# Residual stages of a two-block model: the first step's weights split in two pieces, the source split moved

## The chip, the cores and the metric

The kernel runs on one core of one Trainium2 chip. The metric is the device time in microseconds. TensorE does the matmuls, VectorE, ScalarE and GpSimd the elementwise work, and SyncE issues the loads.

## The reference

The reference is one forward pass over 512 tokens of width 1024, in float32, through two blocks in a row. The first has two layers: a mixer (attention with forgetting and differential heads in layer 0, an mLSTM in layer 1), a cross attention over 256 memory rows and a convolutional feed-forward network of width 2816. The second is a modulated block with a recurrent mixer (rwkv7 and RG-LRU) and a mixture of 32 experts. What matters here is the form in which each of these parts comes back into the residual stream:

```python
x = x + mixed @ w_out                                    # mixers of layers 0 and 1
x = x + cross @ wo[layer]                                # cross attentions
x = x + hidden @ w_down[layer]                           # feed-forward networks, 2816 rows
x = x + gt1[:, None, :] * (merged @ w_out[l])            # second block, gated
mod = c_act @ w_ada[l] + b_ada[l]                        # modulation: 64 columns of 128 values, from one row c
```

## The kernel before, in words

All activations are kept feature-major: 128 partitions, 8 tiles of 512 tokens. The program is a sequence of stages, each a block in which every engine has its own instruction stream; a stage begins for all engines when the one ahead has ended. `stage_dense_residual` (line 449) runs seven times: behind the attention, the mLSTM and the two cross attentions (`src` is `mix`, 8 steps), behind the two feed-forward networks (`src` is `hidden`, 22 steps, `columns` given), and behind the merge of the second block (`src` is `merged`, 8 steps, `gate` given).

A step is one tile of 128 source rows. Its weights are 128x1024 and its source 128x512. TensorE multiplies in a rounded type (float32r), so each operand is split in a rounded half (`hi`) and the rest (`lo`), and each product is three matmuls: hi by hi, hi by lo, lo by hi (`split_products`, lines 220 to 222). A step has 8 output banks and so 24 matmuls of 128x512.

Per step k, on buffer k % 2: ScalarE waits until TensorE has finished step k-2 (`used`) and until the weights have landed, then rounds the weights (line 508) and the source (line 509). GpSimd waits for the rounded weights and makes their rest (line 517). The source's rest (line 478) is VectorE's in the stages without modulation, and GpSimd's, behind the weights' rest, in the two with it. TensorE waits for both rests. SyncE loads the weights of step k once the weights' rest of step k-2 is made (`w_split`). The first and the last round of two steps are written out, the others are in a loop.

Beside the two feed-forward stages runs the `Modulation` (line 1579): 33 and 31 rows of 128x1024 are loaded into three places, and VectorE multiplies each by the row c and sums (line 1619). SyncE's queue issues them in a fixed order: weights of the even step, two rows, weights of the odd step, one row. Before, ScalarE applies Silu to c, behind its work for the first two steps. When all is done, VectorE adds each bank to x (line 553, gated 555).

Of the kernel before, what the change touches and what calls it, by code (L numbers as in the profile page):

```python
# [19 lines left out]
ACT = mybir.ActivationFunctionType  # L20
ALU = mybir.AluOpType
# [5 lines left out]
P = 128  # L27
T = 512
D = 1024
# [81 lines left out]
def first_loads(sp, units):  # L111

    if units is not None:
        for s in range(units.per):
            units.load(sp, 0, s)
# [102 lines left out]
def split_products(nc, out, left, right, first, last):  # L218

    nc.tensor.matmul(out, left.hi, right.hi, start=first, stop=False)  # L220
    nc.tensor.matmul(out, left.hi, right.lo, start=False, stop=False)  # L221
    return nc.tensor.matmul(out, left.lo, right.hi, start=False, stop=last)  # L222
# [226 lines left out]
def stage_dense_residual(g, units, coming, src, gate=None, columns=None):  # L449


    nc = g.nc
    units.begin()
    rounds = units.n
    with ExitStack() as ctx:
        sem, sb = g.stage(ctx, f"dense{units.base[0]}")
        w_rounded, s_rounded, w_split, s_split, used, done, read, passed = (
            sem(n) for n in ("w_rounded", "s_rounded", "w_split", "s_split", "used", "product_done", "bank_read", "passed"))
        w = [Split(sb(f"w_hi{b}", [P, D], F32R), sb(f"w_lo{b}", [P, D], F32R)) for b in range(2)]
        s = [Split(sb(f"s_hi{b}", [P, T], F32R), sb(f"s_lo{b}", [P, T], F32R)) for b in range(2)]  # L460
        beside = Modulation(g, ctx, *columns) if columns else None
        block = ctx.enter_context(nc.Block())

        def steps(eng, step, between=None):

            def both(i):
                for b in range(2):
                    k = 2 * i + b
                    step(i, b, k, slice(k, k + 1) if isinstance(i, int) else bass.ds(k, 1))
            both(0)  # L470
            if between:
                between(eng)
            with eng.Fori(1, rounds - 1) as i:
                both(i)
            both(rounds - 1)

        def rest_of_source(eng, b, tile):
            eng.tensor_tensor(s[b].lo[:, :], src[:, tile, :].rearrange("p a n -> p (a n)"), s[b].hi[:, :],  # L478
                              ALU.subtract).then_inc(s_split, 1)

        @block.sync
        def _(sp):
            def both(i, more=()):
                for b in range(2):
                    sp.wait_ge(w_split, 2 * i + b - 1)
                    units.load(sp, i, b)
                    for s in more[2 * b:2 * b + 2]:
                        beside.load(sp, i, s)
            if beside:
                places = range(beside.PLACES)  # L490
                beside.first_loads(sp)
                with sp.Fori(1, beside.rounds) as i:
                    both(i, places)
                for i in range(beside.rounds, rounds):
                    both(i, places[0:beside.n - beside.PLACES * i])
            else:
                with sp.Fori(1, rounds) as i:
                    both(i)
            sp.wait_ge(w_split, 2 * rounds)
            first_loads(sp, coming)  # L500

        @block.scalar
        def _(act):
            def step(i, b, k, tile):
                if not isinstance(i, int) or i > 0:
                    act.wait_ge(used, k - 1)
                units.wait(act, i, b)
                nc.scalar.activation(w[b].hi[:, :], units.rows(b, 0, D, 0, D), ACT.Copy).then_inc(w_rounded, 1)  # L508
                nc.scalar.activation(s[b].hi[:, :], src[:, tile, :].rearrange("p a n -> p (a n)"), ACT.Copy).then_inc(s_rounded, 1)  # L509
            steps(act, step, beside.scalar if beside else None)  # L510

        @block.gpsimd
        def _(pool):
            def step(i, b, k, tile):
                pool.wait_ge(w_rounded, k + 1)
                pool.sem_inc(passed, 1)
                nc.gpsimd.tensor_tensor(w[b].lo[:, :], units.rows(b, 0, D, 0, D), w[b].hi[:, :], ALU.subtract).then_inc(w_split, 1)  # L517
                if beside:
                    pool.wait_ge(s_rounded, k + 1)
                    pool.sem_inc(passed, 1)  # L520
                    rest_of_source(nc.gpsimd, b, tile)
            steps(pool, step)

        @block.tensor
        def _(pe):
            def step(i, b, k, tile):
                first = isinstance(i, int) and k == 0
                last = isinstance(i, int) and k == 2 * rounds - 1
                pe.wait_ge(w_split, k + 1)
                pe.wait_ge(s_split, k + 1)  # L530
                for m in range(KT):
                    mm = split_products(nc, g.bank[m][:, :], w[b].cut(m * P, (m + 1) * P), Split(s[b].hi[:, :], s[b].lo[:, :]), first, last)
                    if last:
                        mm.then_inc(done, 1)
                if not last:
                    mm.then_inc(used, 1)
            steps(pe, step)

        @block.vector
        def _(dve):  # L540
            def step(i, b, k, tile):
                dve.wait_ge(s_rounded, k + 1)
                dve.sem_inc(passed, 1)
                rest_of_source(nc.vector, b, tile)
            if beside:
                beside.vector(dve)
            else:
                steps(dve, step)
            for m in range(KT):
                dve.wait_ge(done, m + 1)  # L550
                here = g.x[:, m, :]
                if gate is None:
                    nc.vector.tensor_tensor(here, g.bank[m][:, :], here, ALU.add).then_inc(read, 1)
                else:
                    nc.vector.scalar_tensor_tensor(here, g.bank[m][:, :], gate[:, m:m + 1], here, ALU.mult, ALU.add).then_inc(read, 1)
            if beside:
                beside.end(dve)
# [2534 lines left out]
def build(nc, A, where, out):  # L3092

    with ExitStack() as ctx:
        g = Core(nc, ctx, A, where)
        U = {name: Units(g.ring, A[name]) for name in A if name.startswith("w_")}
        stage_setup(g, U["w_attn"])
        stage_attention(g, U["w_attn"], U["w_attn_out"])
        stage_dense_residual(g, U["w_attn_out"], U["w_xattn0"], g.mix)
        for layer in range(2):  # L3100
            if layer == 1:
                stage_mlstm(g, U["w_mlstm"], U["w_mlstm_out"])
                stage_dense_residual(g, U["w_mlstm_out"], U["w_xattn1"], g.mix)
            stage_cross_attention(g, U[f"w_xattn{layer}"], U[f"w_xattn_out{layer}"], layer)
            stage_dense_residual(g, U[f"w_xattn_out{layer}"], U[f"w_up{layer}"], g.mix)
            with nc.sbuf_tensor(f"hidden{layer}", [P, FT, T], F32) as hidden:
                stage_ffn_up(g, U[f"w_up{layer}"], U[f"w_down{layer}"], layer, hidden)
                stage_dense_residual(g, U[f"w_down{layer}"], U[("w_mlstm", "w_rec_in")[layer]], hidden,
                                     columns=((0, 33), (33, 31))[layer])
# [34 lines left out]
```

## Time and profile before

| | |
|---|---|
| median of 3 runs | 2915.34 us (2911.96 to 2918.43) |
| profiled execution, its own time | 2913.45 us |
| its span | 2911.6 us, 38111 instructions |
| TensorE matmuls | 2553.2 us busy (88%) |
| VectorE | 1212.1 us (42%) |
| ScalarE | 957.0 us (33%) |
| GpSimd | 981.3 us (34%) |
| lines 220 to 222 of the residual stages | 672 matmuls each, 270.5 + 266.8 + 266.5 us |

The span is the time from the first to the last instruction of one profiled execution, and its own time is that of the same run measured outside. Busy time of TensorE counts overlapping matmuls, whose ends are modelled, so 88% is not a share of its peak.

### The profile page before, as it was taken

The numbers are of one execution on the slowest core, as the hardware profiler recorded it, in microseconds if no ns is written. First come the engines' busy times: TensorE is split into PE (matmuls) and PEld (weight loads), VectorE is DVE, ScalarE is ACT, GpSimd is POOL, SyncE is SP. The second block draws the span as 40 slices with busy tenths as digits, with TensorE's granted clock in tenths as the row PEclk, the third lists the DMA queues.
The fourth block names the chain that finished last, engine by engine and source line by source line (L and its number), as shares of the span: only waits on it lengthen the run. The fifth ranks groups of instructions, "written<-read, shape, count | busy, mean of one in ns | idle before, by whom it ended". The sixth has DMA issues, their size and how long they took to land. (4 is left out here: it accounts for less than half of the span.)

```text
span 2911.6 us, 38111 instructions
## 1 busy us (share of the span) xinstructions
PE 2553.2 (88%) x14762; PEld 1857.3 (64%) x14762; DVE 1212.1 (42%) x1578; ACT 957.0 (33%) x1362; POOL 981.3 (34%) x469
## 2 busy tenths in 40 slices
PE   8998898899898899789889989889887798579996
PEld 5776786688775666568668877667576586223334
DVE  5443523566554433352256655432644414311112
ACT  4443422444423333243244442243422322201113
POOL 5221422343375311142234337532121342223321
PEclk9999899899998888899989999989999899689998
DMA  3111221222264111122122326422001122598992
GB/s 122 66 44 51 94 87 58 96 91 101 97 227 152 44 43 43 36 105 90 54 91 86 101 80 233 149 72 79 2 4 46 54 77 80 214 370 330 370 349 97
DMA packets 76277, 333.84 MB, mean 115 GB/s; under 512 B 17113, under 2 KB 21209, under 8 KB 51801
## 3 DMA queue, kind: packets, MB, share of 16 engines
q1 hardware_dynamic: 62336, 313.98, 29.7%
q0 software_dynamic: 13824, 18.19, 1.8%
q8 instruction: 87, 1.43, 0.2%
q14 instruction: 30, 0.25, 0.0%
HBM read 372.67 MB, written 16.78 MB: 134 GB/s over the span
## 5 line engine op out<-in xcount | busy, mean ns | idle before, releaser
L517 POOL TENSOR_TENSOR dense_w_lo<-weights,dense_w_hi 128x1024 fp32r<-128x1024 f32 x84 | 203.1, 2420 | 468.4 <-ACT dense_w_hi L508 468.4
L220 PE MATMUL bank<-dense_s_hi,dense_w_hi 128*128 128x512 f32 x672 | 270.5, 402 | 63.5 <-DVE dense_s_lo L478 35.5
L221 PE MATMUL bank<-dense_s_lo,dense_w_hi 128*128 128x512 f32 x672 | 266.8, 397 | 0.0
L222 PE MATMUL bank<-dense_s_hi,dense_w_lo 128*128 128x512 f32 x672 | 266.5, 397 | 0.0
L508 ACT ACTIVATE dense_w_hi<-weights 128x1024 fp32r<-128x1024 f32 x84 | 88.9, 1058 | 345.4 <-PE bank L222 318.7
L220 PEld LDWEIGHTS bank<-dense_s_hi,dense_w_hi 128*128 128x128 f32 x672 | 129.6, 193 | 104.6 <-POOL dense_w_lo L517 39.3
L1276 DVE TENSOR_TENSOR hidden<-up_y 128x512 f32 x44 | 158.2, 3594 | 64.6 <-ACT up_y L1238 64.0
L222 PE MATMUL bank<-xn_r,weights_r 128*128 128x512 f32 x448 | 177.0, 395 | 0.0
L1619 DVE SCALAR_TENSOR_TENSOR xn<-mix,xn 128x1024 f32<-128x1024 f32 x64 | 123.1, 1923 | 118.0 <-DMA mix<-in_modulation 104.6
L2777 PE MATMUL bank<-moe_weights,mix 128*64 128x512 f32 x320 | 151.9, 628 | 17.5 <-DMA experts_more_up<-in_experts_up,moe_more_up 17.3
L1253 POOL TENSOR_TENSOR mix_r<-weights,mix_r 128x2048 fp32r<-128x2048 f32 x22 | 101.3, 4605 | 162.3 <-ACT mix_r L1226 162.3
L220 PE MATMUL bank<-xn_r,mix_r 128*128 128x512 f32 x352 | 141.8, 403 | 8.3 <-DVE up_xn_lo_r L317 8.1
L1253 POOL TENSOR_TENSOR up_w_lo<-weights,up_w_hi 128x2048 fp32r<-128x2048 f32 x22 | 101.3, 4605 | 136.0 <-ACT up_w_hi L1226 136.0
L222 PEld LDWEIGHTS bank<-dense_s_hi,dense_w_lo 128*128 128x128 f32 x672 | 129.2, 192 | 27.9
L221 PEld LDWEIGHTS bank<-dense_s_lo,dense_w_hi 128*128 128x128 f32 x672 | 129.8, 193 | 26.2
L222 PE MATMUL bank<-xn_r,mix_r 128*128 128x512 f32 x352 | 140.2, 398 | 0.0
L221 PE MATMUL bank<-up_xn_lo_r,mix_r 128*128 128x512 f32 x352 | 139.8, 397 | 0.0
L222 PE MATMUL bank<-xn_r,up_w_lo 128*128 128x512 f32 x352 | 139.6, 396 | 0.0
L220 PE MATMUL bank<-xn_r,up_w_hi 128*128 128x512 f32 x352 | 139.0, 395 | 0.0
L221 PE MATMUL bank<-up_xn_lo_r,up_w_hi 128*128 128x512 f32 x352 | 137.4, 390 | 0.0
L2777 PE MATMUL bank<-experts_more_up,mix 128*64 128x512 f32 x256 | 123.3, 638 | 5.1 <-DMA experts_more_up<-in_experts_up,moe_more_up 5.1
L478 DVE TENSOR_TENSOR dense_s_lo<-mix,dense_s_hi 128x512 fp32r<-128x512 f32 x32 | 78.2, 2452 | 112.1 <-ACT dense_s_hi L509 112.1
(637 smaller groups left out, 6082.3 us busy)
## 6 DMA issues: line engine op xcount, KB each, us to landing
weights<-in_w_up SPq DMA_DIRECT2D x44, 1024.0 KB, 4.8
moe_weights<-in_experts_up SPq DMA_DIRECT2D x40, 1024.0 KB, 14.5
mix<-in_modulation SPq DMA_DIRECT2D x64, 512.0 KB, 4.6
weights<-in_w_xattn SPq DMA_DIRECT2D x24, 1024.0 KB, 4.9
weights<-in_experts_up SPq DMA_DIRECT2D x24, 1024.0 KB, 9.4
weights<-in_w_down SPq DMA_DIRECT2D x44, 512.0 KB, 3.7
moe_weights<-in_experts_down SPq DMA_DIRECT2D x40, 512.0 KB, 9.2
weights<-in_w_attn SPq DMA_DIRECT2D x8, 1536.0 KB, 6.6
```

The lines of the kernel that those rows point to most:

```text
L220: nc.tensor.matmul(out, left.hi, right.hi, start=first, stop=False)
L221: nc.tensor.matmul(out, left.hi, right.lo, start=False, stop=False)
L222: return nc.tensor.matmul(out, left.lo, right.hi, start=False, stop=last)
L478: eng.tensor_tensor(s[b].lo[:, :], src[:, tile, :].rearrange("p a n -> p (a n)"), s[b].hi[:, :], ALU.subtract).then_inc(s_split, 1)
L508: nc.scalar.activation(w[b].hi[:, :], units.rows(b, 0, D, 0, D), ACT.Copy).then_inc(w_rounded, 1)
L517: nc.gpsimd.tensor_tensor(w[b].lo[:, :], units.rows(b, 0, D, 0, D), w[b].hi[:, :], ALU.subtract).then_inc(w_split, 1)
L1253: nc.gpsimd.tensor_tensor(w[s].lo, units.rows(s, 0, KT * W, 0, KT * W), w[s].hi, ALU.subtract).then_inc(w_split, 1)
L1276: nc.vector.tensor_tensor(h[:, bass.ds(2 * i + b // 2, 1), :], y[:, b - 1, :], y[:, b, :], ALU.mult).then_inc(h_done, 1)
L1619: g.nc.vector.scalar_tensor_tensor(self.product, self.rows[j % self.PLACES], 1.0, self.c, ALU.mult, ALU.mult, accum_out=g.mod[:, self.firs ...
L2777: mm = nc.tensor.matmul(g.bank[2 + n % 2][half, :], xt[n % 2][:, k, half], w[k // 4][:, k % 4 * 2 * FE:(k % 4 + 1) * 2 * FE], start=(k == ...
```

## The change

In every residual stage the first step is prepared in another order. ScalarE rounds the source first, and then the weights in two pieces, columns 0 to 255 and 256 to 1023 (`PIECES`). GpSimd makes the weights' rest piece by piece, each behind its own count (`w_first_rounded`, `w_first`), and then raises `w_split`. VectorE makes the source's rest, also in the two stages beside the modulation, where GpSimd did it before. TensorE waits for the source's rest (`s_first`) and for the first piece, and for the second piece at output bank 2.

In the later steps of the two stages beside the modulation, ScalarE rounds the source ahead of the weights, and GpSimd makes the source's rest ahead of the weights' rest. In the later steps of the other stages only the counts differ (`s_split` reaches one less, since the first step has its own).

```diff
--- before.py
+++ after.py
@@ -459,7 +459,12 @@
         w = [Split(sb(f"w_hi{b}", [P, D], F32R), sb(f"w_lo{b}", [P, D], F32R)) for b in range(2)]
         s = [Split(sb(f"s_hi{b}", [P, T], F32R), sb(f"s_lo{b}", [P, T], F32R)) for b in range(2)]
         beside = Modulation(g, ctx, *columns) if columns else None
+        w_first, w_first_rounded, s_first = sem("w_first"), sem("w_first_rounded"), sem("s_first")
+        PIECES = ((0, 2 * P), (2 * P, D))
         block = ctx.enter_context(nc.Block())
+
+        def source(tile):
+            return src[:, tile, :].rearrange("p a n -> p (a n)")
 
         def steps(eng, step, between=None):
 
@@ -474,9 +479,8 @@
                 both(i)
             both(rounds - 1)
 
-        def rest_of_source(eng, b, tile):
-            eng.tensor_tensor(s[b].lo[:, :], src[:, tile, :].rearrange("p a n -> p (a n)"), s[b].hi[:, :],
-                              ALU.subtract).then_inc(s_split, 1)
+        def rest_of_source(eng, b, tile, ready):
+            eng.tensor_tensor(s[b].lo[:, :], source(tile), s[b].hi[:, :], ALU.subtract).then_inc(ready, 1)
 
         @block.sync
         def _(sp):
@@ -501,24 +505,47 @@
 
         @block.scalar
         def _(act):
+            def round_source(b, tile):
+                nc.scalar.activation(s[b].hi[:, :], source(tile), ACT.Copy).then_inc(s_rounded, 1)
+
             def step(i, b, k, tile):
                 if not isinstance(i, int) or i > 0:
                     act.wait_ge(used, k - 1)
-                units.wait(act, i, b)
-                nc.scalar.activation(w[b].hi[:, :], units.rows(b, 0, D, 0, D), ACT.Copy).then_inc(w_rounded, 1)
-                nc.scalar.activation(s[b].hi[:, :], src[:, tile, :].rearrange("p a n -> p (a n)"), ACT.Copy).then_inc(s_rounded, 1)
+                if isinstance(i, int) and k == 0:
+                    round_source(b, tile)
+                    units.wait(act, i, b)
+                    for c0, c1 in PIECES:
+                        nc.scalar.activation(w[b].hi[:, c0:c1], units.rows(b, 0, D, c0, c1), ACT.Copy).then_inc(w_first_rounded, 1)
+                    act.sem_inc(w_rounded, 1)
+                elif beside:
+                    round_source(b, tile)
+                    units.wait(act, i, b)
+                    nc.scalar.activation(w[b].hi[:, :], units.rows(b, 0, D, 0, D), ACT.Copy).then_inc(w_rounded, 1)
+                else:
+                    units.wait(act, i, b)
+                    nc.scalar.activation(w[b].hi[:, :], units.rows(b, 0, D, 0, D), ACT.Copy).then_inc(w_rounded, 1)
+                    round_source(b, tile)
             steps(act, step, beside.scalar if beside else None)
 
         @block.gpsimd
         def _(pool):
             def step(i, b, k, tile):
-                pool.wait_ge(w_rounded, k + 1)
-                pool.sem_inc(passed, 1)
-                nc.gpsimd.tensor_tensor(w[b].lo[:, :], units.rows(b, 0, D, 0, D), w[b].hi[:, :], ALU.subtract).then_inc(w_split, 1)
-                if beside:
+                first = isinstance(i, int) and k == 0
+                if beside and not first:
                     pool.wait_ge(s_rounded, k + 1)
                     pool.sem_inc(passed, 1)
-                    rest_of_source(nc.gpsimd, b, tile)
+                    rest_of_source(nc.gpsimd, b, tile, s_split)
+                if first:
+                    for n, (c0, c1) in enumerate(PIECES):
+                        pool.wait_ge(w_first_rounded, n + 1)
+                        nc.gpsimd.tensor_tensor(w[b].lo[:, c0:c1], units.rows(b, 0, D, c0, c1), w[b].hi[:, c0:c1],
+                                                ALU.subtract).then_inc(w_first, 1)
+                    pool.wait_ge(w_first, len(PIECES))
+                    pool.sem_inc(w_split, 1)
+                else:
+                    pool.wait_ge(w_rounded, k + 1)
+                    pool.sem_inc(passed, 1)
+                    nc.gpsimd.tensor_tensor(w[b].lo[:, :], units.rows(b, 0, D, 0, D), w[b].hi[:, :], ALU.subtract).then_inc(w_split, 1)
             steps(pool, step)
 
         @block.tensor
@@ -526,9 +553,14 @@
             def step(i, b, k, tile):
                 first = isinstance(i, int) and k == 0
                 last = isinstance(i, int) and k == 2 * rounds - 1
-                pe.wait_ge(w_split, k + 1)
-                pe.wait_ge(s_split, k + 1)
+                if first:
+                    pe.wait_ge(s_first, 1)
+                else:
+                    pe.wait_ge(s_split, k)
+                    pe.wait_ge(w_split, k + 1)
                 for m in range(KT):
+                    if first and m * P in (c0 for c0, _ in PIECES):
+                        pe.wait_ge(w_first, [c0 for c0, _ in PIECES].index(m * P) + 1)
                     mm = split_products(nc, g.bank[m][:, :], w[b].cut(m * P, (m + 1) * P), Split(s[b].hi[:, :], s[b].lo[:, :]), first, last)
                     if last:
                         mm.then_inc(done, 1)
@@ -541,8 +573,9 @@
             def step(i, b, k, tile):
                 dve.wait_ge(s_rounded, k + 1)
                 dve.sem_inc(passed, 1)
-                rest_of_source(nc.vector, b, tile)
+                rest_of_source(nc.vector, b, tile, s_first if isinstance(i, int) and k == 0 else s_split)
             if beside:
+                step(0, 0, 0, slice(0, 1))
                 beside.vector(dve)
             else:
                 steps(dve, step)
```

## Rows read from the trace of the kernel before

**Rows 1.** The page's costliest groups, busy, mean ns, idle before and releaser:
```profile
L220 PE MATMUL bank<-dense_s_hi,dense_w_hi 128*128 128x512 f32 x672 | 270.5, 402 | 63.5 <-DVE dense_s_lo L478 35.5
```

**Rows 2.** Tile dense_s_hi, idle until: us, times.
```profile
  POOL dense_s_lo L478: 27.8, 22
```

**Rows 3.** Timeline behind the attention: start us, us, engine, line, idle before.
```profile
260.67 1.06 ACT L508 ACTIVATE dense_w_hi<-weights 128x1024 fp32r<-128x1024 f32 x1 [0.29 <-PEq L587]
261.63 0.61 ACT L509 ACTIVATE dense_s_hi<-mix 128x512 fp32r<-128x512 f32 x1
261.91 5.12 POOL L517 TENSOR_TENSOR dense_w_lo<-weights,dense_w_hi 128x1024 fp32r<-128x1024 f32 x2 [51.86 <-ACT dense_w_hi L508]
...
262.40 5.17 DVE L478 TENSOR_TENSOR dense_s_lo<-mix,dense_s_hi 128x512 fp32r<-128x512 f32 x2 [5.17 <-ACT dense_s_hi L509]
...
264.95 0.77 PE L220 MATMUL bank<-dense_s_hi,dense_w_hi 128*128 128x512 f32 x1 [5.20 <-DVE dense_s_lo L478]
```

**Rows 4.** Timeline, start of the gated stage.
```profile
2418.31 1.06 ACT L508 ACTIVATE dense_w_hi<-weights 128x1024 fp32r<-128x1024 f32 x1 [14.18 <-DMA weights<-in_w_mix_out]
...
2422.58 0.77 PE L220 MATMUL bank<-dense_s_hi,dense_w_hi 128*128 128x512 f32 x1 [7.99 <-DVE dense_s_lo L478]
```

**Rows 5.** Timeline, start of the first stage beside the modulation.
```profile
786.43 1.06 ACT L508 ACTIVATE dense_w_hi<-weights 128x1024 fp32r<-128x1024 f32 x1 [2.40 <-PEq L1179]
...
789.96 1.27 POOL L478 TENSOR_TENSOR dense_s_lo<-hidden,dense_s_hi 128x512 fp32r<-128x512 f32 x1
...
791.37 0.77 PE L220 MATMUL bank<-dense_s_hi,dense_w_hi 128*128 128x512 f32 x1 [8.68 <-POOL dense_s_lo L478]
791.87 2.77 DVE L1619 SCALAR_TENSOR_TENSOR xn<-mix,xn 128x1024 f32<-128x1024 f32 x1 [5.74 <-ACT xn L1610]
...
797.57 0.33 SPq L93 DMA_DIRECT2D weights<-in_w_down  x1
```

**Rows 6.** Timeline of ScalarE, two steps apart, behind the first cross attention.
```profile
478.75 1.06 ACT L508 ACTIVATE dense_w_hi<-weights 128x1024 fp32r<-128x1024 f32 x1 [8.41 <-PE bank L222]
...
489.63 1.06 ACT L508 ACTIVATE dense_w_hi<-weights 128x1024 fp32r<-128x1024 f32 x1 [3.95 <-PE bank L222]
```

**Rows 7.** Timeline of a later step beside the modulation.
```profile
834.56 1.06 ACT L508 ACTIVATE dense_w_hi<-weights 128x1024 fp32r<-128x1024 f32 x1 [4.90 <-PE bank L222]
...
835.80 2.39 POOL L517 TENSOR_TENSOR dense_w_lo<-weights,dense_w_hi 128x1024 fp32r<-128x1024 f32 x1 [1.78 <-ACT dense_w_hi L508]
...
837.24 2.03 DVE L1619 SCALAR_TENSOR_TENSOR xn<-mix,xn 128x1024 f32<-128x1024 f32 x1 [2.12 <-DMA mix<-in_modulation]
...
838.14 2.27 POOL L478 TENSOR_TENSOR dense_s_lo<-hidden,dense_s_hi 128x512 fp32r<-128x512 f32 x1
...
838.96 0.93 SPq L1606 DMA_DIRECT2D mix<-in_modulation  x2
...
840.55 0.47 PE L220 MATMUL bank<-dense_s_hi,dense_w_hi 128*128 128x512 f32 x1 [0.66 <-POOL dense_s_lo L478]
...
846.38 1.06 ACT L508 ACTIVATE dense_w_hi<-weights 128x1024 fp32r<-128x1024 f32 x1 [4.88 <-PE bank L222]
```

**Rows 8.** A 128x256 ScalarE activation (timeline); subtractions of line 317, ns min/median/max.
```profile
242.61 0.38 ACT L779 ACTIVATE attention_probs_T<-bank 128x256 f32<-128x256 f32 x1 [0.59 <-PE bank L698]
...
L317 DVE TENSOR_TENSOR xattn_xn_lo_r<-xattn_xn_lo,xn_r x8: 691/693/694, 336.9 to 1297.2; 128x512 fp32r<-128x512 f32 x8
```

**Rows 9.** Stretches: us, TensorE busy (x), granted clock, DMA share, GB/s.
```profile
260.00:264.92 4.92, 0.00 (x0) 0.78 0.00 0
264.92:269.70 4.78, 4.75 (x11) 0.51 0.66 201
...
466.40:471.58 5.18, 0.00 (x1) 0.94 0.00 0
```

**Rows 10.** Loads beside the modulation, KB each, median us to landing.
```profile
mix<-in_modulation SPq DMA_DIRECT2D x33, 512.0 KB, 4.7
weights<-in_w_down SPq DMA_DIRECT2D x20, 512.0 KB, 3.7
```

## The prediction

> **What bounds the kernel now.** I read the page's costliest groups first, then who waited for the source's rounded half, then the timeline at the start of each residual stage, then the clock by stretch, and last the timeline of two steps beside the modulation. The core works through stages one after another; a residual stage ends with its last matmul and the eight adds behind it, so a microsecond gained by TensorE in a stage is a microsecond of the span. TensorE stands at 88% of the span. The first of the three products of a residual stage (line 220) has 63.5 us of idle time ahead of it, 35.5 of them until VectorE's source rest is there [rows 1] and 27.8, in 22 times, until GpSimd's is there [rows 2]. These two are the waits on which the edit works.
>
> The 35.5 us are the starts of the five stages without modulation. Part of each idle time is the end of the stage ahead; what the stage itself costs is counted from ScalarE's first instruction. Behind the attention that is 260.67, and the first matmul is at 264.95: 4.28 us, in which ScalarE rounds 1024 columns of weights, then the source, GpSimd makes the weights' rest and VectorE the source's [rows 3]. In the gated stage the start is the arrival of the weights at 2418.31, and the matmul comes 4.27 us later [rows 4]. The 27.8 us are, in each of the two stages beside the modulation, one start of 8.68 us (4.94 of it behind ScalarE's first instruction, 786.43 to 791.37 [rows 5]) and ten later waits, 20 in both, of (27.8 - 17.4) / 20 = 0.52 us on average.
>
> These later waits come every second step. Without modulation two steps take 489.63 - 478.75 = 10.88 us, so 48 matmuls at 0.227 us [rows 6]. Beside it they take 846.38 - 834.56 = 11.82 us [rows 7]. The 0.94 us between them is the wait and a few slower matmuls behind it. The chain is short and visible: ScalarE starts at 834.56, GpSimd's weights at 835.80, its source rest at 838.14 lasting 2.27 us, the matmul at 840.55, so 5.99 us from ScalarE to TensorE, of which 1.0 us is not work: the same instruction took 1.27 us at 789.96, when VectorE was idle [rows 5], and here VectorE's modulation row stands from 837.24 to 839.27 across its start [rows 7]. GpSimd and VectorE take turns.
>
> **The change at the start of a stage without modulation.** Let ScalarE's first instruction stand at 0. Now the source is rounded first: 0.61 us. VectorE starts 0.16 us behind it (262.40 against 261.63 + 0.61 [rows 3]), at 0.77, and needs 0.69 us when GpSimd is idle, as the same subtraction of 128x512 does elsewhere [rows 8], so it is done at 1.46. In rows 3 two of them needed 5.17 us, since GpSimd was already at work when they began; here VectorE is there first. ScalarE starts the next instruction 0.10 us before the one ahead of it ends (261.63 against 260.67 + 1.06), so the piece of 256 columns stands at 0.51 and ends at 0.89, with the 0.38 us of another 128x256 activation [rows 8]. GpSimd could start 0.18 us later (261.91 against 261.73) at 1.07. I take it that it waits for VectorE until 1.46. Its price for 256 columns: 512 took 1.27 us [rows 5], 1024 took 2.39 [rows 7], so 2.1 to 2.2 ns a column and 0.2 fixed: 0.73 us for 256 and 1.8 for 768. The piece is there at 2.19, and TensorE starts 0.14 later, as at 791.23 to 791.37 [rows 5]: **2.33 instead of 4.28, 1.95 us less.** Four stages (behind the attention, the mLSTM and both cross attentions): 7.8 us. The bounds: GpSimd isn't held, 1.96 instead of 2.33 (2.3 less); or the small instruction has as much fixed time as the whole 128x512 one, 1.27 us, and is held as well (1.4 less).
>
> The row at 838.14 shows the turn-taking, and it bears on the order of the first two. The Trainium skill (page "SBUF — State Buffer", section "SBUF: two separate sides") calls the pair of ports that the two engines share an exclusive lock: whoever starts first keeps it for the whole instruction. By that rule GpSimd's first piece waits for 1.46; if the two merely shared it would not, and the sum for six starts would be 6 x 0.37 = 2.2 us larger.
>
> Does the second piece hold TensorE? It runs 2.2 to 4.05. The first six matmuls need only the first piece. The clock was at its lower level (1.2 GHz) in all of the first 4.78 us of this stage, 11 matmuls at 0.43 us [rows 9], so six last 2.6 us, to 4.9: no wait. At 2.4 GHz they last 1.4, to 3.7, and TensorE waits 0.4. Step two: its source rest and then its weights' rest follow on GpSimd until some 7.1, and TensorE needs them at 2.33 + 7.4 or, with the upper clock, at 8.2: hidden. The weights of step three are asked for when the first rest is whole, at 4.2 (before at 3.8), land 3.7 us later [rows 10] at 7.9 and are needed behind step one, at 8.0 at the earliest (2.33 + 5.45 and ScalarE's start): hidden, at the upper clock barely.
>
> **In the gated stage** the source is rounded and its rest made before the weights land; nothing holds GpSimd. From the landing: 0.38 + 0.18 + 0.73 + 0.14 = 1.43 instead of 4.27, **2.8 us less**.
>
> **The starts beside the modulation.** GpSimd had weights' rest and source rest of step one in a row. The source rest goes to VectorE, idle until 791.87 [rows 5]: 2.33 instead of 4.94, **2.6 us less, twice 5.2**. What is moved: VectorE's first row, behind ScalarE's Silu at 5.4, now meets GpSimd's weights' rest of step two (5.4 to 7.8) instead of its source rest, and is perhaps 0.8 us later; the next load of weights on SyncE's queue stands behind that row's reload, at 797.57 [rows 5], and lands near 801.3, while step four's ScalarE work would be due at about 801.9 with TensorE 2.6 us earlier. Hidden, by little; if not, up to 1 us a stage.
>
> **The later steps beside the modulation.** From ScalarE's start, without a row of VectorE in between: 0.61 + 0.18 + 1.27 + 2.40 + 0.14 = 4.6 us. Before, the same sum was 1.06 + 0.18 + 2.40 + 1.27 + 0.14 = 5.05. The matmul at 840.55 started 0.66 + 0.39 = 1.05 us behind the one ahead of it instead of 0.23, so it lost 0.82, and without a wait it would stand 5.99 - 0.82 = 5.17 us behind ScalarE's start; the other 0.12 of the 0.94 us are the slower matmuls behind the wait. With one modulation row in the way (1.0 us) the new chain is 5.6: a wait of 0.43 instead of 0.82. With none, no wait. With a row ahead of each of GpSimd's two instructions, 6.6: worse than now. So it hangs on when rows land. A row's reload is issued some 0.75 us behind the end of the weights' rest, the weights' own load between them (838.96 against 835.80 + 2.39 [rows 7]), and lands 4.7 us after issue [rows 10]. The weights' rest is now the last link, so everything shifts. Counting from a step's ScalarE start (period 5.45): rest whole at 4.5, first row issued at 5.2, landed at 9.9, which is 4.45 in the next step, under the last of GpSimd's weights' rest; it then runs 1.23 us up to 0.25 in the step behind, before GpSimd's source rest at 0.79. The second of the pair lands some 1.4 us later and runs into that source rest, holding it by about 0.8: chain 5.4, a wait of 0.25 and the slower matmuls' 0.12 once in two steps. The third row finds room. So 0.57 of the 0.94 us goes, ten times in each of two stages: **11.4 us**. Bounds: 0 (a row ahead of the weights' rest each time, late by 0.4 more than I count) to 0.94 (no row in the way), 0 to 19 us. The weights' load comes 0.9 us later in the step and has over 2 us of slack before ScalarE needs it.
>
> **The clock.** Idle time ahead of the stage behind the first cross attention was 5.2 us, with the granted clock at 0.94 on average, so the lower level came only in its last 0.6 us; behind the attention it was 0.78, the last 2.2 us [rows 9]. With 1.95 us less of idleness the first could keep 2.4 GHz: ten matmuls 0.2 us faster, less the 0.4 us wait for piece two, 1.6. Three of the seven stages have so short an idle time, so 0 to 5 us; I take 1. The Trainium skill ("TensorE: Matmul & The Clock Gate", Part 1) says that the monitor runs free of the program, so where the level changes varies from run to run; by it this term is luck in every stage. The 0.6 and 2.2 us of two like stages agree.
>
> **The sum.** 7.8 + 2.8 + 5.2 + 11.4 + 1.0 = 28.2 us. The profiled execution took 2913.45 us around a span of 2911.6, 1.9 under the median of 2915.34; it would come to 2885.3, and the median to **2887**. No other stage is touched, and each starts as before, only earlier. What a measurement of this kernel can tell from no change is about 0.2%, 5.8 us.
>
> **Rivals.**
> 1. The starts gain, the later steps don't: rows land ahead of GpSimd's second instruction, chain 6.0 as before. Gain 10 to 19, about 2900. For it: my count of landings is good to perhaps 0.5 us, and 0.4 decides. Chance 0.20.
> 2. All later waits go and the clock stays up: 7.8 + 2.8 + 5.2 + 18.8 + 4 = 38.6, about 2877. For it: the uncontended chain has half a microsecond to spare. Against it: VectorE holds 3 x 1.23 of each 10.9 us. Chance 0.15.
> 3. Slower: GpSimd now has two places per step where VectorE can slip in ahead of something that TensorE waits for. Where all three rows of two steps hit, one step waits 6.6 - 5.17 = 1.4, the other 0.4, and 0.12 for each: 2.0 instead of 0.94, times 20 = 21 us lost against 16 gained at the starts: 2920. It decides from 0.94 + 15.8 / 20 = 1.7 us of waiting in two steps. Against it: in the row at 837.24 one landing hits one instruction, and three rows that land 1.4 to 5 us apart seldom all do. Chance 0.05.
> 4. It doesn't do what it says: GpSimd keeps the pair when its piece is ready, or small instructions are dear, so that the starts give under 1 us and the steps nothing: within 0.2%. Chance 0.05.
>
> The forecast itself, a gain of 19 to 36, has 0.55. Range: 2868 to 2904, which leaves out rivals 3 and 4 and the far ends of 1 and 2. Faster by over 0.2%: 0.89 (forecast, rivals 1 and 2, less 0.01 for the low end); same 0.06; slower 0.05.
>
> **What would show it.** In the starts: the first matmul 2.3 us after ScalarE's first instruction, 1.4 behind the landing in the gated stage; VectorE's rest of 0.69 us ahead of GpSimd's first piece. In the steps: two steps in 11.2 to 11.3 us instead of 11.82, and the wait now put down to the weights' rest. If two steps take 11.8 or more, the landings are what failed; if the starts show over 3 us, the prices of the pieces or the turn-taking are.

## The result, and the profile after

The changed kernel took 2892.58 us (median of 5 runs, 2887.71 to 2897.01) against 2915.34 (5 runs): a ratio of 0.992, 95% interval 0.9908 to 0.9931, so 22.8 us less. The profiled execution has a span of 2890.4 us against 2911.6. The direction and the starts of the stages came as forecast; the later steps beside the modulation gave a third of what was forecast.

The time of each residual stage, from ScalarE's first instruction (in the gated stage from the landing of its weights) to the end of the last add, read from the two timelines in us ("less" is what the stage became shorter by):

| stage behind | first matmul, before | after | stage, before | after | less |
|---|---|---|---|---|---|
| attention | 4.28 | 2.20 | 50.98 | 48.13 | 2.85 |
| cross attention 0 | 4.28 | 2.20 | 50.13 | 48.02 | 2.11 |
| feed-forward 0 (modulation) | 4.94 | 2.19 | 136.94 | 132.36 | 4.58 |
| mLSTM | 4.28 | 2.20 | 50.72 | 48.02 | 2.70 |
| cross attention 1 | 4.27 | 2.19 | 50.76 | 47.11 | 3.65 |
| feed-forward 1 (modulation) | 4.95 | 2.19 | 135.80 | 131.04 | 4.76 |
| merge (gated) | 4.27 | 1.36 | 50.86 | 48.46 | 2.40 |

That is 23.0 us; the span fell by 21.2, so the stages that the change doesn't touch took 1.8 longer in this execution.

In the page's costliest groups, the first product now waits for GpSimd's first pieces (line 541) where it waited for VectorE [rows 1]; 63.5 us of idle time became 43.6:

```profile
L220 PE MATMUL bank<-dense_s_hi,dense_w_hi 128*128 128x512 f32 x672 | 269.7, 401 | 43.6 <-POOL dense_w_lo L541 36.2
```

The timeline behind the attention answers to rows 3. VectorE's rest takes 0.69 us, since it is ahead of GpSimd; the two pieces (one row, x2) start at 261.55, and TensorE 1.19 us behind that. The two rows at the end are the first piece by itself, here and in the gated stage:

```profile
260.54 0.63 ACT L509 ACTIVATE dense_s_hi<-mix 128x512 fp32r<-128x512 f32 x1 [0.29 <-PEq L620]
261.07 1.13 ACT L518 ACTIVATE dense_w_hi<-weights 128x256 fp32r<-128x256 f32 x2
...
261.32 0.69 DVE L483 TENSOR_TENSOR dense_s_lo<-mix,dense_s_hi 128x512 fp32r<-128x512 f32 x1 [4.22 <-ACT dense_s_hi L509]
261.55 2.82 POOL L541 TENSOR_TENSOR dense_w_lo<-weights,dense_w_hi 128x256 fp32r<-128x256 f32 x2 [51.65 <-ACT dense_w_hi L518]
...
262.74 0.77 PE L220 MATMUL bank<-dense_s_hi,dense_w_hi 128*128 128x512 f32 x1 [3.12 <-POOL dense_w_lo L541]
...
261.55 1.04 POOL L541 TENSOR_TENSOR dense_w_lo<-weights,dense_w_hi 128x256 fp32r<-128x256 f32 x1 [51.65 <-ACT dense_w_hi L518]
2399.70 0.73 POOL L541 TENSOR_TENSOR dense_w_lo<-weights,dense_w_hi 128x256 fp32r<-128x256 f32 x1 [19.24 <-ACT dense_w_hi L518]
```

Behind the second cross attention the clock stayed up, and the second piece was late there: the weight load (PEld) of the third bank waited for it for 0.53 us, and the matmul started 0.49 us behind the one ahead of it (1412.16) instead of 0.23:

```profile
1410.94 0.47 PE L220 MATMUL bank<-dense_s_hi,dense_w_hi 128*128 128x512 f32 x1 [3.11 <-POOL dense_w_lo L541]
...
1412.65 0.19 PEld L220 LDWEIGHTS bank<-dense_s_hi,dense_w_hi 128*128 128x128 f32 x1 [0.53 <-POOL dense_w_lo L541]
```

A usual pair of later steps beside the modulation answers to rows 7. VectorE's row at 829.04 stands ahead of GpSimd's source rest at 829.17, which takes 2.24 us instead of 1.29; the chain from 828.28 to 833.80 is 5.52 us. Two steps take 839.68 - 828.28 = 11.40 us, where they took 11.82:

```profile
828.28 0.63 ACT L509 ACTIVATE dense_s_hi<-hidden 128x512 fp32r x1 [4.34 <-PE bank L222]
...
829.04 1.23 DVE L1652 SCALAR_TENSOR_TENSOR xn<-mix,xn 128x1024 f32<-128x1024 f32 x1 [0.51 <-DMA mix<-in_modulation]
829.17 2.24 POOL L483 TENSOR_TENSOR dense_s_lo<-hidden,dense_s_hi 128x512 fp32r<-128x512 f32 x1 [2.23 <-ACT dense_s_hi L509]
...
831.37 2.38 POOL L548 TENSOR_TENSOR dense_w_lo<-weights,dense_w_hi 128x1024 fp32r<-128x1024 f32 x1
...
833.80 0.50 PE L220 MATMUL bank<-dense_s_hi,dense_w_hi 128*128 128x512 f32 x1 [0.22 <-POOL dense_w_lo L548]
...
839.68 0.63 ACT L509 ACTIVATE dense_s_hi<-hidden 128x512 fp32r x1 [4.38 <-PE bank L222]
```

But three of the nine pairs of feed-forward 0 took 12.3 or 12.4 us (none of feed-forward 1 took over 11.7). In the first of them a row of VectorE is ahead of both of GpSimd's instructions (2.21 us for the source's rest, 3.35 for the weights'), and TensorE waits 1.17 us:

```profile
792.88 1.23 DVE L1652 SCALAR_TENSOR_TENSOR xn<-mix,xn 128x1024 f32<-128x1024 f32 x1
793.05 2.21 POOL L483 TENSOR_TENSOR dense_s_lo<-hidden,dense_s_hi 128x512 fp32r<-128x512 f32 x1 [2.70 <-ACT dense_s_hi L509]
...
795.11 1.23 DVE L1652 SCALAR_TENSOR_TENSOR xn<-mix,xn 128x1024 f32<-128x1024 f32 x1 [0.99 <-DMA mix<-in_modulation]
795.22 3.35 POOL L548 TENSOR_TENSOR dense_w_lo<-weights,dense_w_hi 128x1024 fp32r<-128x1024 f32 x1
...
798.62 0.50 PE L220 MATMUL bank<-dense_s_hi,dense_w_hi 128*128 128x512 f32 x1 [1.17 <-POOL dense_w_lo L548]
```

The groups of GpSimd in feed-forward 0 give the sum of the holds, that is, of the time by which VectorE made its instructions longer (busy us, mean ns). Before, the held instruction was the source's rest alone:

```profile
L517 POOL TENSOR_TENSOR dense_w_lo<-weights,dense_w_hi 128x1024 fp32r<-128x1024 f32 x22 | 52.8, 2399 | 50.0 <-ACT dense_w_hi L508 50.0
L478 POOL TENSOR_TENSOR dense_s_lo<-hidden,dense_s_hi 128x512 fp32r<-128x512 f32 x22 | 46.0, 2092 | 0.0
```

After, both are:

```profile
L548 POOL TENSOR_TENSOR dense_w_lo<-weights,dense_w_hi 128x1024 fp32r<-128x1024 f32 x21 | 57.0, 2716 | 0.0
L483 POOL TENSOR_TENSOR dense_s_lo<-hidden,dense_s_hi 128x512 fp32r<-128x512 f32 x21 | 38.7, 1842 | 27.1 <-ACT dense_s_hi L509 26.9 <-POOL dense_w_lo L541 0.3
```

Against what the two cost when VectorE leaves them alone (2401 and 1293 ns, e3 below), GpSimd was held 22 x 0.80 = 17.6 us before and 21 x (0.32 + 0.55) = 18.1 after. There the change moved the holds and took none away. In feed-forward 1 the same sum went from 15.6 us (22 of 2403 and 2001 ns) to 12.7 (21 of 2623 and 1674).

### The profile page after: what moved, and what is told of

It reads as the page before. It is cut to its first block and busy times, and to the rows that moved or that the text cites. A ratio compares the mean times of both kernels' runs of the same rounds, so it can differ in the third digit from the quotient of the medians.

```text
span 2890.4 us, 38084 instructions
## 1 busy us (share of the span) xinstructions
PE 2551.0 (88%) x14762; PEld 1857.5 (64%) x14762; DVE 1172.4 (41%) x1580; ACT 958.5 (33%) x1369; POOL 978.5 (34%) x474
## 5 line engine op out<-in xcount | busy, mean ns | idle before, releaser
L220 PE MATMUL bank<-dense_s_hi,dense_w_hi 128*128 128x512 f32 x672 | 269.7, 401 | 43.6 <-POOL dense_w_lo L541 36.2
L548 POOL TENSOR_TENSOR dense_w_lo<-weights,dense_w_hi 128x1024 fp32r<-128x1024 f32 x77 | 196.6, 2554 | 97.1 <-ACT dense_w_hi L526 95.7
L1652 DVE SCALAR_TENSOR_TENSOR xn<-mix,xn 128x1024 f32<-128x1024 f32 x64 | 100.2, 1566 | 134.1 <-DMA mix<-in_modulation 124.2
L1265 ACT ACTIVATE up_y<-bank,vecs 128x512 f32<-128x512 f32 x88 | 68.5, 779 | 169.3 <-PE bank L222 159.2
L541 POOL TENSOR_TENSOR dense_w_lo<-weights,dense_w_hi 128x256 fp32r<-128x256 f32 (+1 forms) x14 | 19.5, 1411 | 293.8 <-ACT dense_w_hi L518 293.8
```

The costliest lines, as they stand in the source:

```text
L541: nc.gpsimd.tensor_tensor(w[b].lo[:, c0:c1], units.rows(b, 0, D, c0, c1), w[b].hi[:, c0:c1], ALU.subtract).then_inc(w_first, 1)
L1265: nc.scalar.activation(y[:, b, :], g.bank[b][:, :], ACT.Identity, scale=tap(2, i, b), bias=tap(3, i, b)).then_inc(now_done, 1)
L1652: g.nc.vector.scalar_tensor_tensor(self.product, self.rows[j % self.PLACES], 1.0, self.c, ALU.mult, ALU.mult, accum_out=g.mod[:, self.firs ...
```

## The experiments

Theory A says that the starts made nearly all of the gain, and that VectorE's rows, in GpSimd's way, kept the later steps from giving more. Theory B says that the two parts gave shares as forecast. Rivals C and D are stated where they are tested. e1 to e4 ran beside one set of runs of the kernel before (2914.80 us), e5 to e7 beside another (2917.29).

What was expected of each run stands in front of its result, as it was written before the run.

**e1, the starts alone**, and **e2, the order alone**, each one part of the change (excerpts, with notes behind #; the expectation of e1 comes first):

```diff
 e1, from the kernel after:                       # ScalarE and GpSimd, steps k > 0
-                elif beside:
-                    round_source(b, tile)        # source ahead of weights
...
 e2, from the kernel before:
+                source_ahead = beside and not (isinstance(i, int) and k == 0)
+                if source_ahead:                 # ScalarE: source, weights; GpSimd likewise
```

> Only the first steps are changed; the later steps beside the modulation keep the order of before (weights, then source, on ScalarE and GpSimd). Theory A (the starts made nearly all of the 22.8 us, the later steps some 4): 2915.3 - 19 = 2896 us, and two later steps beside the modulation take 11.8 us as before. Theory B (the two parts gave about equal shares, as 16.8 to 11.4 in the forecast): 2915.3 - 13 = 2902. Both: first matmul 2.2 us behind ScalarE's first instruction in six stages.

> The kernel before, with only the order of source and weights turned in the later steps beside the modulation; all first steps as before. Theory A: a gain of 2 to 5 us (about 2911), two steps mostly in 11.4 us, with single pairs of 12 and more where VectorE's rows stand ahead of both of GpSimd's instructions. Theory B: a gain of 10 us, 2905.

e1: 2897.75 us, ratio 0.9938 (0.9921 to 0.9955), 18 us less by the ratio (13 to 23). e2: 2908.47 us, ratio 0.9982 (0.9971 to 0.9992), 5 us less (2 to 8). The parts add up to the whole (18 + 5 = 23), as far as intervals of 5 and 3 us to each side can tell, and in the shares of theory A. Theory B's 13 us for e1 stand at the edge of its interval; it is e2 that leaves out theory B's 10 us, and the 11.4 of the forecast.

The expectation for e1's pairs held only in part. Most took 11.7 to 11.9 us, three 12.1 to 12.3, and one of feed-forward 0 15.3. Two things met in it. With the rows nearly back to back, GpSimd's instructions were held one after the other (weights' rest 3.35 us, source rest 2.26), and TensorE waited 2.45 us at 807.22. And from 808.54 to 811.95 TensorE was at 1.2 GHz (granted clock 0.50, last row), ten matmuls that cost about 1.6 us more than at 2.4. ScalarE then waited 8.15 us:

```profile
807.06 3.35 POOL L540 TENSOR_TENSOR dense_w_lo<-weights,dense_w_hi 128x1024 fp32r<-128x1024 f32 x1
...
810.05 1.43 DVE L1648 SCALAR_TENSOR_TENSOR xn<-mix,xn 128x1024 f32<-128x1024 f32 x1 [1.87 <-DMA mix<-in_modulation]
810.37 2.26 POOL L483 TENSOR_TENSOR dense_s_lo<-hidden,dense_s_hi 128x512 fp32r<-128x512 f32 x1
...
814.63 1.06 ACT L522 ACTIVATE dense_w_hi<-weights 128x1024 fp32r<-128x1024 f32 x1 [8.15 <-PE bank L222]
...
807.22 0.49 PE L220 MATMUL bank<-dense_s_hi,dense_w_hi 128*128 128x512 f32 x1 [2.45 <-POOL dense_s_lo L483]
...
808.54:811.95 3.41, 3.41 (x10) 0.50 0.29 95
```

In that execution feed-forward 0 was 2.0 us longer than before (138.94 against 136.94) although its first matmul was 2.75 us earlier. In e2, where TensorE starts as late as before, all eighteen pairs of the two stages took 11.3 to 11.6 us. The 19 later steps, from ScalarE's start in the third to that in the last, took in the two stages:

| kernel | start | order | feed-forward 0 | feed-forward 1 |
|---|---|---|---|---|
| before | late | old | 111.87 | 111.26 |
| e1 | early | old | 116.15 | 112.40 |
| e2 | late | new | 108.04 | 108.47 |
| after | early | new | 110.79 | 108.55 |

So in feed-forward 0 the earlier start made the later steps longer, by 4.3 us with the old order (about 1.6 of it by the clock, as above) and by 2.8 with the new. The single pairs of 12 us that I expected in e2 are not there; in feed-forward 0 they are where the start was moved forward. Each of these figures is from one profiled execution. GpSimd was held less in e2, too: 12.0 us in feed-forward 0 (22 of 2564 and 1675 ns) and 13.2 in feed-forward 1 (2699 and 1597).

**e3, short rows**: VectorE's rows keep their loads and waits, but compute 64 of 1024 columns.

```diff
-            g.nc.vector.scalar_tensor_tensor(self.product, self.rows[j % self.PLACES], 1.0, self.c, ...
+            g.nc.vector.scalar_tensor_tensor(self.product[:, 0:64], self.rows[j % self.PLACES][:, 0:64], 1.0, self.c[:, 0:64], ...
```

> The kernel after, with VectorE's modulation instructions cut to the first 64 of their 1024 columns (this leaves out most of the modulation sums); all loads, waits and counts stay. Theory A (VectorE's rows hold the SBUF access from GpSimd, and that is the rest of the loss in the later steps): two steps beside the modulation in 10.9 us, 19 steps some 7 us shorter in each of the two stages, so 2892.6 - 14 = 2879. Rival C (what holds the later steps is the landing of the loads, which keep their size): two steps stay at 11.4 us, 2890 to 2893.

The 19 later steps took 103.26 us in both stages, pairs of 10.9 throughout, and GpSimd's two instructions their bare time:

```profile
L548 POOL TENSOR_TENSOR dense_w_lo<-weights,dense_w_hi 128x1024 fp32r<-128x1024 f32 x21 | 50.4, 2401 | 0.0
L483 POOL TENSOR_TENSOR dense_s_lo<-hidden,dense_s_hi 128x512 fp32r<-128x512 f32 x21 | 27.2, 1293 | 36.8 <-ACT dense_s_hi L509 36.5 <-POOL dense_w_lo L541 0.3
```

The two stages are 7.9 and 5.3 us shorter than in the kernel after, 13.2 for the 14 expected, with the loads the same in number and size, if not in time: rival C (the loads) falls. The time as a whole, 2859.65 us, fell by 33, more than the stages explain: what follows the gated stage took 426.2 us of the span instead of 442.7. The incomplete modulation sums go into the router, and the work of the experts depends on values; that this is the cause of the 16.5 us is inferred, not shown, so e3 is read by its two stages alone.

**e4, the source's rest on VectorE in every step**, between its rows, with ScalarE's weights first again (VectorE's part of the edit):

```diff
-                step(0, 0, 0, slice(0, 1))
-                beside.vector(dve)
+                for k in range(2 * rounds):
+                    step(k // 2, k % 2, k, slice(k, k + 1))
+                    if k == 1:
+                        dve.wait_ge(beside.silu_ready, 1)
+                        beside.multiply(dve, range(0, 3))
+                    elif k > 1:
+                        j = 3 * (k // 2) + 2 * (k % 2)
+                        beside.multiply(dve, range(j, min(j + 2 - k % 2, beside.n)))
```

> The kernel after, but in the two stages beside the modulation VectorE makes the source's rest in every step, between its rows (two rows behind the rest of an even step, one behind that of an odd step), and ScalarE rounds the weights first again. GpSimd has only the weights' rest. Chain of GpSimd from ScalarE's start 1.06 + 0.18 + 2.39 + 0.14 = 3.8 us, 4.9 with one row ahead of it, under the 5.2 us that it has. Theory A: two steps in 10.9 us, 2892.6 - 13 = 2880. Rival C (loads): no gain. Rival D (VectorE comes late to the source's rest, because it stands behind a row that has not landed): two steps over 11.4 us, 2893 or more.

2880.29 us (2877.82 to 2883.79), ratio 0.9881 (0.9867 to 0.9896). The forecast of 2880 held. In the pair shown, GpSimd is ahead and takes 2.40 us, as in nearly every step; VectorE's rest waits for it (2.46 us) and is done at 830.56, before TensorE wants it. Pairs are 837.26 - 826.38 = 10.88 us:

```profile
826.38 1.06 ACT L522 ACTIVATE dense_w_hi<-weights 128x1024 fp32r<-128x1024 f32 x1 [3.95 <-PE bank L222]
...
827.61 2.40 POOL L540 TENSOR_TENSOR dense_w_lo<-weights,dense_w_hi 128x1024 fp32r<-128x1024 f32 x1 [3.13 <-ACT dense_w_hi L522]
828.10 2.46 DVE L483 TENSOR_TENSOR dense_s_lo<-hidden,dense_s_hi 128x512 fp32r<-128x512 f32 x1 [1.92 <-ACT dense_s_hi L509]
...
837.26 1.06 ACT L522 ACTIVATE dense_w_hi<-weights 128x1024 fp32r<-128x1024 f32 x1 [3.94 <-PE bank L222]
```

The stages are 124.60 and 124.44 us, as short as with short rows (124.43, 125.77), with all the work done, and TensorE waits ahead of none of their later steps. So the holds fell on the path only because GpSimd had two instructions in the chain. Rival D falls too.

**e5, one piece**: source first, VectorE ahead, but the weights whole.

```diff
-        PIECES = ((0, 2 * P), (2 * P, D))
+        PIECES = ((0, D),)
```

> The kernel after with the first step's weights in one piece of 1024 columns; the source still goes first and its rest to VectorE. Theory A (the piece is what brings the start forward, since GpSimd's 1024 columns of 2.4 us stand last in the chain): first matmul 0.51 + 1.06 + 0.18 + 2.39 + 0.14 = 4.3 us behind ScalarE's first instruction in six stages, as much as before; 2892.6 + 6 x 2.1 + 2.4 = 2907 us. Rival B (the order, source first and VectorE ahead of GpSimd, brings it): first matmul 2.2 to 2.8 us, 2893 to 2897.

2903.75 us, ratio 0.9953 (0.9939 to 0.9966). The first matmul is 4.14 us behind ScalarE's first instruction in six stages, so without the piece the start is not brought forward to 2.20:

```profile
260.81 0.63 ACT L509 ACTIVATE dense_s_hi<-mix 128x512 fp32r<-128x512 f32 x1 [0.28 <-PEq L620]
...
262.46 2.34 POOL L541 TENSOR_TENSOR dense_w_lo<-weights,dense_w_hi 128x1024 fp32r<-128x1024 f32 x1 [52.19 <-ACT dense_w_hi L518]
...
264.95 0.77 PE L220 MATMUL bank<-dense_s_hi,dense_w_hi 128*128 128x512 f32 x1 [5.06 <-POOL dense_w_lo L541]
```

The order alone gives 0.14 us in four stages, 0.8 in the two beside the modulation (4.95 before) and 0.65 in the gated one (3.62 behind the landing). Pieces in the old order were not run, so what they give without the source going first is not shown.

The time is 3 us under the expected 2907. With the later start nearly every pair beside the modulation was regular again (19 steps in 108.23 and 107.86 us), as in e2, while I had counted on those of the kernel after.

**e6, three pieces on top of e4**:

```diff
-        PIECES = ((0, 2 * P), (2 * P, D))
+        PIECES = ((0, P), (P, 3 * P), (3 * P, D))
```

> The kernel of e4 (VectorE makes the source's rest in every step) with the first step's weights in three pieces: 128, 256 and 640 columns. Theory A: a piece of 128 columns costs GpSimd 0.46 us, is ready at 0.28 + 0.51 + 0.18 = 0.97 and held by VectorE until 1.46: first matmul at 1.46 + 0.46 + 0.14 = 2.06 or a little less, instead of 2.20, and 1.1 instead of 1.36 in the gated stage; 7 x 0.2 = 1.4 us less, which the trace shows and the times hardly: 2879. Rival: GpSimd's fixed time per instruction is larger for so small a piece, or a third piece comes late with the clock up, and nothing is gained: 2880 to 2882.

2874.16 us (2871.86 to 2877.32), ratio 0.9854 (0.9839 to 0.9869): the fastest of all. The first matmul is at 1.93 us instead of 2.20 in six stages and 0.99 instead of 1.36 behind the landing, so 2.0 us in all. That the median is 6 us under e4's is more than this explains, and the intervals of the two ratios touch (0.9867 to 0.9869). The two profiled executions are 6.7 us apart, 3.1 of it in the residual stages: 1.7 behind the mLSTM, where e4's TensorE stayed at 1.2 GHz for 15 matmuls and e6's for 7, so by the clock. The other 3.6 us lie in stages that the two kernels share.

**e7, both weights ahead of the rows in SyncE's queue, on top of e4**:

```diff
-                    for s in more[2 * b:2 * b + 2]:
-                        beside.load(sp, i, s)
+                for s in more:
+                    beside.load(sp, i, s)
```

> The kernel of e4 with SyncE's queue beside the modulation turned: both weights of a round first, then its three rows. In e4 ScalarE waited 5.0 and 3.5 us for the weights of steps three and four, whose loads stood beside or behind the first rows' reloads; the stage lost about 2 us by it. Theory A: the second of these waits shrinks by 2 us or more, and 0 to 2 us are gained in each stage: 2878. Rival: the rows now land a step later, VectorE waits for them ahead of the source's rest, and two steps rise over 10.9 us: 2885 or more.

2877.70 us, ratio 0.9874 (0.9856 to 0.9892), not told apart from e4. Feed-forward 0 lost both of ScalarE's waits for weights (8.5 us in sum in e4), feed-forward 1 kept one of 4.7, and the stages took 124.45 and 124.44 us against 124.60 and 124.44. The 2 us that I had put down to ScalarE's waits for these loads are not there: the waits were hidden, and cost TensorE nothing that can be seen here. Pairs stayed at 10.9, so its rival falls as well.

## Why the forecast held, point by point

**Starts without modulation**: 1.95 us each was forecast, with the first matmul at 2.33; it is 2.20, so 2.08. GpSimd's first piece was held as said: it took 1.04 us beside VectorE and 0.73 in the gated stage, where nothing held it, the price worked out for 256 columns. The hold costs less than the 0.46 us by which the two overlap: the piece ends 0.58 us behind VectorE's end at 262.01 and not 0.73, and this accounts for the 0.13 by which 2.33 was too late. The Trainium skill's exclusive lock ("SBUF — State Buffer", "SBUF: two separate sides") fits this but for that 0.15 us: the piece lost 0.31 us to the VectorE instruction that was ahead of it, and a source rest about 1.0 to a modulation row. e5 shows that without the piece the gain is not there. Two small sums of the prediction are off, without effect: the bound without a hold is 1.07 + 0.73 + 0.14 = 1.94 and not 1.96, and the second piece ends at 2.19 + 1.8 = 3.99 and not 4.05.

**Gated stage**: the first matmul came 2.9 us earlier (2.8 forecast); the stage is only 2.4 us shorter, since 13 matmuls were at 1.2 GHz behind it instead of 10.

**Starts beside the modulation**: 2.75 us each (2.6 forecast). The first row is later and the load of step four's weights lands late, at 799.19, 0.97 us behind its due time, as feared. It cost nothing by itself, since GpSimd was held until 800.81 in the source's rest anyway.

**The clock**: 1.0 us was taken, between 0 and 5. The four stages without modulation and the gated one became 13.7 us shorter, their first matmuls 4 x 2.08 + 2.9 = 11.2 earlier; 2.5 us are left, and they are the clock's. Behind the first matmul TensorE was at 1.2 GHz (granted clock 0.50) for 11 matmuls before and 7 after behind the attention, 7 and 7 behind cross attention 0, 10 and 7 behind the mLSTM, 10 and none behind cross attention 1, 10 and 13 in the gated stage. At 0.2 us for each, less the 0.26 us for which TensorE waited for the second piece, that is 2.5 us. So the two errors in the sum have opposite signs, and it is luck that this one went that way.

The prediction had three candidates, the stages behind the attention and the two cross attentions. Behind cross attention 1 the clock stayed at 2.4 GHz, and the stage was 0.9 us shorter than its like (47.11 against 48.02). In the other two it fell, in the last 0.4 and 0.6 us of an idle time that is the same in all three, 3.11 to 3.12 us (each stretch begins where the last matmul ended):

```profile
259.62:262.74 3.12, 0.00 (x1) 0.94 0.00 0
262.74:265.60 2.86, 2.86 (x7) 0.50 0.00 0
464.67:467.79 3.12, 0.00 (x1) 0.90 0.00 0
467.79:470.60 2.81, 2.81 (x7) 0.50 0.00 0
...
1407.83:1410.94 3.11, 0.00 (x0) 1.00 0.00 0
```

The prediction called this luck in every stage. In the profiled executions of the six kernels with the two or three pieces (the kernel after, e1, e3, e4, e6, e7) these three stages always came out alike: at 1.2 GHz behind the attention and cross attention 0, at 2.4 behind cross attention 1. Behind the mLSTM it varied: e4's stage took 49.63 us, that of the others 47.9 to 48.1.

**Later steps**: this is the term that was mis-sized. 11.4 us was forecast (0.57 of 0.94 us in each of 20 pairs), and the profile shows 1.1 + 2.7 = 3.8. What there was to gain is 16.6 us (111.87 and 111.26 against the 103.26 of e3) and not 18.8. The usual pair came near: 11.40 instead of 11.82, so 0.42, with the chain at 5.52 us (5.4 forecast) and one row ahead of the source's rest, as worked out. In e2, where every pair is as short as this, the 19 steps gave 3.8 + 2.8 = 6.6 us (the times give 5, at most 8). So 4.8 of the missing 7.6 us are missing even there, by sizes, and the other 2.8 where the start is early. Two things failed. "The third row finds room" did not hold: in the irregular pairs a row stands ahead of the weights' rest too. And these come in feed-forward 0 where the start is early (e1, the kernel after) and hardly where it is late (e2, e5), so the two parts of the edit don't merely add up in feed-forward 0: the earlier start gave 2.75 us, and some of what the order would give was lost again to the rows' new places. Why the rows fall there, whether by the first row's hold of 3.30 us at 788.14 or by the loads' later landing (5.2 us instead of 4.7 [rows 10]), I did not separate.

The measured 22.8 lies between the forecast's 28.2 and the first rival's 10 to 19 (starts gain, later steps don't). The usual chain is the forecast's (5.52 us) and not that rival's (6.0), and the third rival, a row ahead of each of GpSimd's instructions, showed itself in single pairs. The sum of 28.2 was 5.4 above the measured 22.8: 11.4 against 3.8 in the later steps, and 8.8 against 11.3 in the four starts with the clock.

## What to carry to other kernels

When TensorE waits at the head of a stage, look for the longest instruction of the last link and cut off only the part that the first matmuls read: here 256 of 1024 columns, with the source first, gave 2.08 of 4.28 us, and 128 gave 2.35. To turn the order within a chain whose engine is held by another mostly moves the holds (in feed-forward 0 from 17.6 us to 18.1, and to 12.0 with the late start), and the sum of the instructions stays; taking one instruction out of the chain gave 17 us (e4 against e1), where turning the two gave 5. Where two engines hold each other, a forecast of periods from where single loads land is worth about its sign.

## What the hardware showed that was not expected

GpSimd and VectorE took strict turns: a GpSimd instruction that follows another of its own directly still lets a waiting VectorE row in between (3.35 us instead of 2.40 at 795.22), so two instructions in a chain can be held twice, one only once. In none of the nine traces is a weights' rest beside the modulation longer than 3.44 us, so none was held by two rows.

The length of the idle time did not tell what TensorE's clock would do. After 3.12 us without a matmul it had fallen to 1.2 GHz in two stages and stood at 2.4 GHz in a third. In e6 the idle time is 2.85 us in the same three stages, and behind cross attention 0 the clock fell 2.64 us after the last matmul. In e4 and e7 it fell behind the attention only when TensorE was at work again, 0.51 and 0.27 us behind the first matmul (granted clock 1.00 until 263.90 in e4, 0.50 from there to 267.31).
